# Value blocks of a differential-attention kernel: the 128x128 turn on TensorE replaced by 32x32 turns on VectorE and a regrouping load

## The reference

```
h = rms_norm(x, norm_pre) * (1 + scale) + shift
q, k, v, z = h @ w_in            # 4 slices of 2048 columns each
p = softmax(where(mask, q_m @ k_m / sqrt(128), -1e30))     # for m = 0, 1
attn = p_0 - lam * p_1
o = rms_norm(attn @ v, subln) * 0.8 * silu(z)
x + gate * rms_norm(o @ w_out, norm_post)
```

## Time and profile before

| | |
|---|---|
| median of 3 runs | 1907.58 us (1907.35 to 1908.47) |
| the profiled execution | 1907.34 us, of which the span of instructions is 1905.5 us |
| PE busy | 1866.0 us, 98% |
| DVE busy | 1379.5 us, 72% |
| ACT busy | 810.1 us, 43% |
| POOL busy | 794.4 us, 42% |
| DMA, mean busy share of 16 engines by SP's queue | 76.4% |
| mean granted TensorE clock | 0.999 |

### The profile page before, as it was taken

One profiled execution on the slowest core, in us unless ns is written; L12 is line 12 of the kernel. 1 busy time (PEld: TensorE's weight loads), 2 busy tenths in 40 slices (PEclk: granted clock), 3 DMA queues, 4 the chain that ended last, 5 costly groups with the idle time before them and its releaser, 6 DMA issues.

```text
span 1905.5 us, 26384 instructions
## 1 busy us (share of the span) xinstructions
PE 1866.0 (98%) x9072; PEld 1540.9 (81%) x9072; DVE 1379.5 (72%) x2028; ACT 810.1 (43%) x1516; POOL 794.4 (42%) x844
## 2 busy tenths in 40 slices
PE   4999999999999999999999999999999999999998
PEld 1488888888888888888888888888888888888886
DVE  3687888886655546787887877878778776569467
ACT  5633333333444433444443444444444445546452
POOL 2076565655644523344344434434443422116023
PEclk9999999999999999999999999999999999999999
DMA  9898898886674698786877778686777679657777
GB/s 354 253 313 279 274 297 278 284 290 232 214 267 160 237 356 263 225 250 192 253 229 227 235 216 252 198 254 212 232 240 221 213 228 291 207 186 257 258 240 265
DMA packets 394048, 473.16 MB, mean 248 GB/s; under 512 B 22614, under 2 KB 268476, under 8 KB 391228
## 3 DMA queue, kind: packets, MB, share of 16 engines
q1 hardware_dynamic: 393632, 471.43, 76.4%
q10 hardware_dynamic: 284, 0.05, 0.0%
HBM read 323.54 MB, written 147.86 MB: 247 GB/s over the span
## 4 chain that ended last, share of the span: by engine, by line
PE 93%; DVE 1%; DMA 1%; ACT 0%; issue 0%; SPq 0%; POOL 0%; DVEq 0%; POOLq 0%; ACTq 0%
PE ps L1752 30%; PE ps L1754 30%; PE ps L1753 30%; PE ps L1885 2%; PE ps L1861 1%; PE ps L1904 1%; PE ps L1721 0%; DMA ubf<-s_dr 0%; DMA z_dr<-cc 0%; PE ps L1833 0%; DVE ring L1310 0%; ACT h L1040 0%; DVE xt L1632 0%; DVE tB L1330 0%; DVE tB L1327 0%
## 5 line engine op out<-in xcount | busy, mean ns | idle before, releaser
L1752 PE MATMUL ps<-blk,ring 128*128 128x512 f32 x1524 | 603.3, 396 | 2.6 <-DVE blk L1357 1.9
L1754 PE MATMUL ps<-blk,ring 128*128 128x512 f32 x1524 | 594.6, 390 | 0.0
L1753 PE MATMUL ps<-blk,ring 128*128 128x512 f32 x1524 | 594.2, 390 | 0.0
L1752 PEld LDWEIGHTS ps<-blk,ring 128*128 128x128 f32 x1524 | 286.3, 188 | 66.0 <-issue 9.7
L1754 PEld LDWEIGHTS ps<-blk,ring 128*128 128x128 f32 x1524 | 286.0, 188 | 60.8
L1753 PEld LDWEIGHTS ps<-blk,ring 128*128 128x128 f32 x1524 | 286.5, 188 | 55.8
L1310 DVE TENSOR_TENSOR ring<-sums,ring 128x512 fp32r<-128x512 f32 x256 | 234.7, 917 | 95.5 <-ACT ring L1006 93.6
L836 POOL TENSOR_TENSOR sums<-raw 128x512 f32<-128x512 f32 x128 | 191.5, 1496 | 226.9 <-DVE ring L1310 206.0
L1006 ACT ACTIVATE ring<-sums 128x512 fp32r<-128x512 f32 x256 | 160.6, 628 | 179.3 <-PE ps L1754 175.6
L1310 DVE TENSOR_TENSOR ring<-raw,ring 128x512 fp32r<-128x512 f32 x192 | 179.2, 934 | 58.9 <-ACT ring L1006 58.5
L836 POOL TENSOR_TENSOR sums<-sums,raw 128x512 f32<-128x512 f32 x128 | 190.2, 1486 | 20.8 <-DVE ring L1310 14.3
(11 more groups left out here) (159 smaller groups left out, 3181.7 us busy)
## 6 DMA issues: line engine op xcount, KB each, us to landing
raw<-in_diff_w_in_dram SPq DMA_DIRECT2D x64, 1024.0 KB, 7.8
d_dr<-cc SPq DMA_DIRECT2D x124, 256.0 KB, 3.2
cc<-d_dr SPq DMA_DIRECT2D x124, 256.0 KB, 4.1
ubf<-s_dr SPq DMA_DIRECT2D x113, 256.0 KB, 5.0
ada<-in_ada_w_dram SPq DMA_DIRECT2D x88, 256.0 KB, 7.3
tb<-in_diff_w_out_dram SPq DMA_DIRECT2D x32, 512.0 KB, 5.5
t_dr<-tb SPq DMA_DIRECT2D x32, 512.0 KB, 4.9
ada<-in_ada_w_dram SPq DMA_DIRECT2D x32, 512.0 KB
```

Source lines behind the costliest of these rows:

```text
L1752: MM(dst, a_hi, b_hi, start=start, stop=False, skip_group_check=True)
L1753: MM(dst, a_hi, b_lo, start=False, stop=False, skip_group_check=True)
L1754: return MM(dst, a_lo, b_hi, start=False, stop=stop, skip_group_check=True)
```

## The change

The turn moves from PE to DVE. One `transpose` instruction of DVE on [128, 512] turns each square of 32x32 in its place, so a square's row and column of squares stay where they were. DVE does it one slot after the product that completes the block, behind `post_low` of the block before and ahead of `take`. ACT and DVE read bank 7 as before. The parts are stored as they lie, each partition a row of 512 floats. What is left of the turn, that squares go to their places, is done by the loads: `load_v` becomes four DMAs of 32 partitions each, and a partition's 512 floats come in 16 pieces of 32 floats (128 bytes) from rows that lie 64 KB apart.

```diff
+SIDE = 32
...
-        v_dr = dram("v_dr", [HEADS * SEQ, 2, VD])
+        v_dr = dram("v_dr", [HEADS * 2, 2, 2, P, HALF])
...
                     if part == 2:
-                        dst = v_dr[h * SEQ + half * HALF:h * SEQ + (half + 1) * HALF].rearrange("(t p) s d -> p t s d", p=P)
-                        sp.dma_start(dst[:, :, s, m * P:(m + 1) * P],
-                                     src.rearrange("p (t d) -> p t d", t=HT).bitcast(F32)).then_inc(stored[o], 16)
+                        sp.dma_start(v_dr[h * 2 + half, s, m], src.bitcast(F32)).then_inc(stored[o], 16)
...
-                sp.dma_start(v_sb[:, qb].bitcast(F32),
-                             v_dr[h * SEQ + qb * P:h * SEQ + (qb + 1) * P]).then_inc(v_ld[qb % 2], 16)
+                for c in range(0, P, SIDE):
+                    n = qb % HT * P + c
+                    sp.dma_start(v_sb[c:c + SIDE, qb].rearrange("i s (c j) -> i (s c) j", j=SIDE).bitcast(F32),
+                                 v_dr[h * 2 + qb // HT, :, :, :, n:n + SIDE].rearrange(
+                                     "s m (c i) j -> i (s m c) j", i=SIDE)).then_inc(v_ld[qb % 2], 16)
...
                 if part == 2:
-                    act.wait_ge(vt_mm, 4 * h + o + 1)
+                    act.wait_ge(vt_ok, 4 * h + o + 1)
...
+            def v_turn(n):
+
+                i, pi = divmod(n, NP)
+                h, o = head_part(i)[0], AT[pi]
+                if h or o:
+                    dve.wait_ge(post_d, 12 * h + o if o else 12 * (h - 1) + 4)
+                dve.wait_ge(ev_d, 3 * GP + NP * (i - GP) + pi + 1)
+                V.transpose(ps[:, VX], cc[:, buffer_of(i, BLOCK[pi])]).then_inc(vt_ok, 1)
+
             def posts(n):
                 for w in (n - 2, n - 1):
                     if w >= NA and w % NP in BLOCK and w == n - lag(w):
                         post_low(w)
+                if n - 1 >= NA and (n - 1) % NP in BLOCK and head_part((n - 1) // NP)[1] == 2:
+                    v_turn(n - 1)
...
-            def v_turn(i, pi):
-                h, _ = head_part(i)
-                b, o = BLOCK[pi], AT[pi]
-                pe.wait_ge(*read_out(i, pi))
-                if h or o:
-                    pe.wait_ge(post_d, 12 * h + o if o else 12 * (h - 1) + 4)
-                for t in range(HT):
-                    last = TR(ps[:, VX, t * P:(t + 1) * P], cc[:, buffer_of(i, b), t * P:(t + 1) * P], ident[:, :])
-                last.then_inc(vt_mm, 1)
...
-                pe.wait_ge(v_ld[qb % 2], (a // 2 + 1) * 16)
+                pe.wait_ge(v_ld[qb % 2], (a // 2 + 1) * 16 * (P // SIDE))
```

More of the change, by code:

```diff
@@ L294, in build @@
         d_ld = [sem(f"d_ld{i}") for i in range(CCR)]
-        post_hi, post_d, post_p, vt_mm = sem("post_hi"), sem("post_d"), sem("post_p"), sem("vt_mm")
+        post_hi, post_d, post_p, vt_ok = sem("post_hi"), sem("post_d"), sem("post_p"), sem("vt_ok")
         stored = [sem(f"stored{i}") for i in range(4)]
```

## The result

The changed kernel takes 1919.11 us (median of 4 runs, 1916.43 to 1920.90) against 1907.46 us before: a ratio of 1.0057, with a 95% interval of 1.0044 to 1.0069. It is slower; forecast were 1897.4 us and a range from 1892.8 to 1912. The profiled execution took 1916.43 us with a span of 1914.5 us, 9.1 us over the profiled execution of before. The medians differ by 11.7 us.

A forecast was written before the change was run, and what follows sets the result against it. PE's own instructions were taken to bound the kernel. The profiled 1907.34 - 14.2 (PE) + 0.7 (DVE) + 3.3 (last head's start) gave 1897.1 us, 1897.4 as median; range 1892.8 to 1912.

The forecast's parts named there:

- What leaves PE: 128 transposes in 32 turns leave PE, 0.445 us a turn, saving 14.2 us in full.
- What DVE gains: 32 transposes on DVE at 0.69 us; in query block 2 PE waits 0.1 us in 7 heads, 0.7 us.
- What the transfers gain: Value loads in 128-byte pieces at 12.5 ns, 1.6 us a load; these and three more issues are covered, costed at nothing.
- The last head's start: Six more value-load issues before z's store, three before the next units, delay the chain through SP: 3.3 us.
- the forecast's path: Last head's start: z's store lands, SP loads z, q, k and units, ACT copies `ubf`, then PE's matmul; 3.3 us later.
- (c): Rival for value loads: small pieces are handled twice, 52.8 ns each, DMA engines become the bound: 2041 us; chance 0.12 with prices towards it.
- (d): Rival for DVE: its turn costs 1.5 us, giving 1907.3 us, no change; chance 0.05.
- (b): Rival for transfers: pieces cost 26.4 ns, about 1 us in 7 heads, 10.8 at last head's start: 1911.9 us; 0.17 with its half.
- (a): Rival: the whole gain, last head's start loses nothing and DVE's slack holds: 1893.4 us; chance 0.16.

The follow-up runs named there:

- e14: Changed kernel, but in query block 3 of heads 0 to 6 SP issues the partial sum's load ahead of value, q and k loads and two stores: 1900.69 us.
- e15: Changed kernel with value loads spread a block ahead, the last head's moved, one DVE turn late, and e14's order: 1893.90 us.
- e13: Changed kernel, but query block 3's value loads of heads 0 to 6 stand right behind the partial sum's load: 1908.11 us.
- e11: Changed kernel, but value loads of query blocks 1 to 7 of heads 0 to 6 are issued a block ahead, four together behind the first slot: 1919.97 us.
- e9: Changed kernel, but only query block 3's four value loads are spread over the three slots of query block 2: 1911.59 us.
- e12: Changed kernel, but query block 3's four value loads move together to behind the load of z of query block 2: 1918.11 us.
- e6: Changed kernel, but in the last head the next query block's value loads stand behind the load of z: 1917.46 us.
- e1 to e3: e1, e3 and, between them, the changed kernel with four value loads of 32 whole 2 KB rows per query block: 1908.96 us.
- e3: Changed kernel, but one value load of 2048 pieces of 128 bytes per query block in heads 1 to 7 (whole rows in head 0): 1907.62 us.
- e1: Changed kernel, but one value load of 128 rows of 2 KB per query block, squares left where they lie: 1899.69 us.

## Why the prediction was wrong

Starts of PE's first matmul of `weighted`, less those of the kernel before, in us, read from PE's timelines, show where each part falls:

| head, query block | after | e14 | e15 |
|---|---|---|---|
| 2, 2 | -1.51 | -6.74 | -7.52 |
| 2, 3 | -0.42 | -6.79 | -7.65 |
| 6, 3 | +4.43 | -12.49 | -14.58 |
| 7, 0 | +6.90 | -10.17 | -14.59 |
| 7, 4 | +9.19 | -6.41 | -13.38 |

**What leaves PE: right.** At head 6's block 3 all 32 turns are passed, and in e15, where PE waits for nothing before that, it is 14.58 us ahead. Of these it had 0.36 already ahead of the first turn (its last product matmul there starts at 713.45, for 713.81 before), so the turns are worth 14.2 us, as forecast.

**What DVE gains: the price right, the wait under-sized.** The turn takes 0.72 us for 0.69. PE waits 0.23 us in query block 2 of each of 7 heads, 1.6 us for 0.7 forecast. The timelines of DVE and PE in head 2, to hold against the earlier trace rows:

```profile
1033.25 0.55 DVE L1561 TENSOR_TENSOR aT_lo<-ps,aT_hi 128x384 fp32r<-128x384 f32 x1
...
1033.49 0.39 PE L1767 MATMUL ps<-e,ring 128*128 128x512 f32 x1
1033.94 0.36 PE L1765 MATMUL ps<-v_sb,aT_hi 128*128 128x256 f32 x1
```

`aT_low` ends at 1033.80, before the 1034.00 of the forecast, and PE starts 0.14 us later; the 0.1 us taken for a slack of nearly nothing was too little.

**What the transfers gain: the packets right, the cover wrong.** This is the step that failed: a term put at nothing. It said that three more issues of some 0.4 us are covered, "as SP mostly waits behind the load for PE's scores", and "I cost it at nothing". The value loads themselves were covered: PE never waited for `v_sb`. But the step asked only who waits for the values, not who stands behind them in SP's queue. Behind them stands the load of the partial sum. It cost 14.4 us of waits in 7 heads, and 16.9 us by the table (from -12.49 to +4.43). Of the other 2.5 us, 1.6 are one stretch at half clock (last section), 0.4 lay between the two executions ahead of the first turn, and the last 0.5 are spread over the heads.

Two readings of the trace before would have shown it. First, the cover was measured against the old schedule. SP's idle time behind the value load was 1.69 us, and the new issues take 1.66 us more (2.16 for 0.50), which looks like a fit. But this idle time is a wait for PE's scores, and the change makes PE earlier: the last score matmul starts at 1036.25 instead of 1037.68. So q's load could have left 1.43 us sooner; it left at 1038.33, 0.22 later than before. The gain and the cover were the same time, counted twice. Second, this load already ended last in the old trace: `take` of P5 waited 0.21 us for it in head 2, and PE started `weighted` 0.14 us late behind it:

```profile
1044.98 0.69 DVE L1468 TENSOR_TENSOR cc<-ps,cc 128x512 f32<-128x512 f32 x1 [0.21 <-DMA cc<-d_dr]
```

In the list of waits this is 0.2 us, once, on DVE; on PE's side it is not listed at all. In this head the chain had no slack.

**The last head's start: place right, half of the path wrong, under-sized.** PE loses 4.7 us there in the profiled execution of the changed kernel (from +4.52 at the end of head 6 to +9.19) and 6.1 in e14, which arrives earlier; forecast were 3.3. Other executions with the same program in this head lose 5.9 (e13), 6.4 (e11), 7.5 (e9) and 8.0 us (e12), so one execution does not give the size. In the changed kernel the first 2.4 us come sooner than the forecast's path: z's store lands at 1573.80, but PE has waited before that. Behind the eight value loads stand the units' loads, ACT waits for one of them, DVE for ACT, and DVE's `aT_low` comes behind this:

```profile
1569.36 1.06 ACT L1179 ACTIVATE ub<-ubf 128x1024 fp32r<-128x1024 f32 x1 [4.95 <-DMA ubf<-s_dr]
...
1570.44 1.23 DVE L1602 TENSOR_TENSOR ub<-ubf,ub 128x1024 fp32r<-128x1024 f32 x1 [2.57 <-ACT ub L1179]
...
1572.02 0.36 PE L1765 MATMUL ps<-v_sb,aT_hi 128*128 128x256 f32 x1 [2.38 <-DVE aT_lo L1561]
```

In e6, with four value loads there instead of eight, this wait is gone. The rest runs as forecast, over the value loads to z's store, against the earlier trace rows:

```profile
1559.84 0.32 SPq L556
...
1566.90 1.05 SPq L524
1567.99 5.81 DMA z_dr<-cc
1573.93 0.36 SPq L567
...
1591.59 4.92 DMA q_sb<-q_dr
...
1597.45 0.47 PE ps L1765
```

Of what follows, the forecast had the value loads of the next block, 1.2 us more for three more issues; the four at 1578.79 took 4.2 us, where the single load of the kernel before took 0.65. The four at 1587.06 were not in it. Both push q's load on, for which PE then waits 1.3 us at 1597.45; and behind the wait of 2.38 us the clock was at half for a stretch (last section).

**The rivals.** (c) is out: small pieces aren't handled as if twice. The Trainium skill (DMA: Bandwidth & Descriptors, Specifications) says that below 512 bytes an engine does a read-modify-write; with the 12.8 ns per 128-byte packet measured here against 26.4 ns for a 512-byte one, no such penalty is seen for these loads into SBUF. (d) is out by the 0.72 us. (b) named the right place, "the partial sums' loads behind the stores come late", and its 1911.9 us is the nearest of the forecasts. But it hung this on a packet price of 26.4 ns, which did not hold, and gave it 1 us a head where 2.1 us were lost. (a), the whole gain at 1893.4 us, is about what e15 reaches with 1893.90, and only with its other changes.

**What is shown and what stays open.** e14 shows that the place of one load in SP's queue makes the loss in the heads, as it changes nothing else and PE's wait in block 3 is 0.0 us with it; e1 to e3 show that more issues and smaller pieces each push it. Not settled is why some issues of value loads take 1 to 3 us where the median is 0.5 (maximum 3.1 us in the changed kernel), and where the other executions of the changed kernel spend the 2.7 us by which the median exceeds the profiled one; the last head's start, with 4.7 to 8.0 us in the profiles, is one candidate.

## What to carry to other kernels

In this kernel a transfer that was split or cut into small pieces was paid for by what stood behind it in its queue, not by who waits for its data; so list the next issues of the queue and find the one whose data is wanted first. Idle time that ends when the bottleneck engine delivers is no cover for a change that makes that engine faster: measure slack against the new schedule. When such a loss shows, first move the late, urgent load ahead (18.4 us here for one line's order), before reshaping or moving the bulky ones.

## What the runs showed of the hardware

- The clock can fall behind a short wait, and the price comes on top. After PE's wait of 2.45 us that ended at 1157.99 in the changed kernel, the stretch behind it ran partly at the lower level. Window of that stretch (us, busy of each engine, granted clock, DMA share), PE's timeline in it, and at the end the window behind the longest wait, of 2.74 us, that ended at 825.94:

```profile
1158.00:1161.00 3.00, 3.00 (x18) 3.00 (x19) 1.04 (x2) 1.08 (x3) 0.38 (x2) 0.72 0.72 142
...
1160.18 0.47 PE L1767 MATMUL ps<-k_sb,q_sb 128*128 128x320 f32 x1
1160.45 0.47 PE L1765 MATMUL ps<-k_sb,q_sb 128*128 128x320 f32 x1
...
826.00:832.00 6.00, 6.00 (x37) 5.51 (x38) 4.19 (x9) 3.37 (x8) 2.36 (x5) 1.00 0.66 159
```

Starts of 320-column matmuls lie 0.27 us apart, which is 1.2 GHz, and between query blocks 3 and 4 of this head 1.6 us were lost. The Trainium skill (TensorE: Matmul & The Clock Gate, Part 1: The HAM clock gate) gives the same two levels, and that cold start-to-start time is the columns over 1.2 GHz; 320 / 1.2 = 267 ns agrees. After the wait of 2.38 us that ended at 1572.02, the five 512-column matmuls from 1573.91 on started 427 ns apart. But behind the waits of 2.74 us (1.00 in the last row) and of 2.41 us, that ended at 1492.19, the granted clock stayed at the full level. So of PE's four waits of 2.4 to 2.7 us two were followed by the lower level and two were not: the length of a wait alone does not tell.
- Behind one load of 2048 small pieces the next issue on the queue took 1.11 us (median) instead of 0.37, though the load's own issue took 0.50 at the median (e3 against e1).
- The loads in pieces of 128 bytes, each from another row of memory, moved at 12.8 ns a packet, and the heads' DMA share rose by only 0.07.
